# Four modulation slabs of each layer: out of the attention block, into the norm ahead of the FFN

## What is computed

```python
def layer(x, cond, p, l, angles, ctx):
    mod = jax.nn.silu(cond) @ p['w_mod'][l] + p['b_mod'][l]
    sh1, sc1, g1, sh2, sc2, g2 = jnp.split(mod, 6, axis=-1)
    h = rms_norm(x, p['norm1'][l]) * (1.0 + sc1) + sh1
    mixed, ctx_out = token_mixers(h, p, l, angles, ctx)
    x = x + g1 * mixed
    h = rms_norm(x, p['norm2'][l]) * (1.0 + sc2) + sh2
    a, u = jnp.split(h @ p['w_ffn_in'][l], 2, axis=-1)
    x = x + g2 * ((jax.nn.silu(a) * u) @ p['w_ffn_out'][l])
    return x, ctx_out
```

## Time and profile before

| | |
|---|---|
| median of 3 runs | 2581.82 us (2580.06 to 2582.97) |
| the profiled execution | 2584.01 us, its span 2582.1 us |
| PE busy | 2415.1 us, 94% of the span |
| DVE / ACT / POOL busy | 54% / 37% / 18% |
| mean granted clock of PE | 0.968 of full speed |
| read from HBM | 206.46 MB, 82 GB/s over the span |

### The profile page before, as it was taken

How to read it: one execution, slowest core, us unless ns; L and a number is a source line. 1 busy time by engine, 2 the same in 40 slices (tenths; PEclk the granted TensorE clock), 3 DMA queues, 4 the chain that set the end, 5 groups by cost and what they waited for, 6 DMA issues and landing times. The chain is left out here.

```text
span 2582.1 us, 40460 instructions
## 1 busy us (share of the span) xinstructions
PE 2415.1 (94%) x16718; PEld 2237.5 (87%) x16718; DVE 1402.1 (54%) x2040; ACT 943.2 (37%) x1747; POOL 476.2 (18%) x345
## 2 busy tenths in 40 slices
PE   6988989999999899999999799898999989999997
PEld 5767867789999899999997588677999989999997
DVE  3334657642225783866753446676222368568383
ACT  3433346631113442333335233675111234234240
POOL 1241000000003531403335010000000055033130
PEclk9989999999999899999989899999999999999998
DMA  7233233222222132232220521311222222313221
GB/s 217 91 113 125 67 95 128 75 74 74 74 82 82 34 98 67 72 100 59 82 91 19 177 92 38 125 37 34 82 75 80 67 61 71 98 50 98 66 78 62
DMA packets 246197, 213.52 MB, mean 83 GB/s; under 512 B 8928, under 2 KB 231712, under 8 KB 246016
## 3 DMA queue, kind: packets, MB, share of 16 engines
q1 hardware_dynamic: 239696, 208.10, 26.2%
q10 hardware_dynamic: 5808, 2.17, 0.4%
q0 software_dynamic: 512, 0.66, 0.2%
HBM read 206.46 MB, written 4.46 MB: 82 GB/s over the span
## 5 line engine op out<-in xcount | busy, mean ns | idle before, releaser
L2516 DVE TENSOR_TENSOR ring_low<-raw,ring_high 128x512 fp32r<-128x512 f32 (+1 forms) x278 | 268.8, 989 | 102.4 <-ACT ring_high L2413 102.2
L2413 ACT ACTIVATE ring_high<-raw 128x512 fp32r<-128x512 f32 (+1 forms) x278 | 156.8, 609 | 253.3 <-PE ps L2657 211.8
L1537 DVE TENSOR_TENSOR wL<-raw,wH 128x1024 fp32r<-128x1024 f32 (+1 forms) x46 | 79.8, 1736 | 287.4 <-ACT wH L1474 286.7
L2705 PE MATMUL ps<-hH,ring_low 128*128 128x320 f32 x640 | 199.5, 312 | 4.8 <-issue 4.8
L2705 PE MATMUL ps<-hL,ring_high 128*128 128x320 f32 x640 | 199.0, 311 | 0.0
L2705 PE MATMUL ps<-hH,ring_high 128*128 128x320 f32 x640 | 198.9, 311 | 0.0
L332 PE MATMUL ps<-wH,hL 128*128 128x512 f32 (+1 forms) x460 | 175.6, 382 | 14.7 <-DVEq L998 14.7
L2657 PE MATMUL ps<-gH,ring_low 128*128 128x320 f32 x704 | 165.2, 317 | 18.2 <-DVE gL L2548 18.2
L369 PE MATMUL ps<-hH,wL 128*128 128x320 f32 x768 | 177.9, 313 | 0.0
L369 PE MATMUL ps<-hL,wH 128*128 128x320 f32 x768 | 176.0, 310 | 0.0
L369 PE MATMUL ps<-hH,wH 128*128 128x320 f32 x768 | 175.7, 310 | 0.0
(11 more groups left out here) (328 smaller groups left out, 6089.9 us busy)
## 6 DMA issues: line engine op xcount, KB each, us to landing
raw<-in_w_in SPq DMA_DIRECT2D x56, 1024.0 KB, 5.3
raw<-in_w_ffn_in SPq DMA_DIRECT2D x88, 512.0 KB, 5.0
modw<-in_w_mod SPq DMA_DIRECT2D x24, 1024.0 KB, 5.1
gmod<-in_w_mod SPq DMA_DIRECT2D x16, 1024.0 KB, 7.6
raw<-in_w_ffn_out SPq DMA_DIRECT2D x16, 1024.0 KB, 5.1
raw<-in_w_branch SPq DMA_DIRECT2D x24, 512.0 KB, 3.4
head_w<-in_w_mod SPq DMA_DIRECT2D x8, 1024.0 KB, 11.8
raw<-in_w_out SPq DMA_DIRECT2D x8, 1024.0 KB, 5.6
```

Source lines behind the costliest of these rows:

```text
L1537: nc.vector.tensor_tensor(m.wL[:, slot, 0:n], m.raw[:, slot, 0:n], m.wH[:, slot, 0:n].bitcast(F32), ALU.subtract).then_inc(m.sem("low_read ...
L2413: nc.scalar.activation(ring_block(m.ring_high, b, src.shape[1], src.shape[2]), src, ACT.Copy).then_inc(m.sem("w_high"), 1)
L2516: nc.vector.tensor_tensor(ring_block(m.ring_low, b, nk, cols), src, ring_block(m.ring_high, b, nk, cols).bitcast(F32), ALU.subtract).then_ ...
L2705: last = nc.tensor.matmul(m.ps[:, plan.banks[n, i][0], 0:HALF], w[:, k, :], a[:, k, :], start=(k == 0 and q == 0), stop=(k == 3 and q == 2))
```

## The change

Of the 8 slabs of its own layer that an attention block computed, it now computes 4 (16 to 19, the rest of sh2 and sc2); those of the next layer stay. Slabs 20 to 23 (g2) are loaded at the start of the tail into four buffers of their own (`fmod`), by SP ahead of slab 2 of w_out, and are multiplied by PE inside the norm: two ahead of the sums over channels, two between these and the spread. ACT copies the two rows of results (`f_row`) ahead of and behind its root. PE turns them by 8 small matmuls behind the last tile of slab 4, DVE adds the bias ahead of its first FFN multiplication, and PE waits for that addition before the second tile of slab 5.

```diff
@@ tail, sync @@
             for j in range(2):
                 sp.sem_inc(m.sem(f"slab_loaded{j}"), 16)
+            for j in range(4):
+                sp.dma_start(m.fmod[j][:, :, :], k_tiles(d["w_mod"], L, (20 + j) * W256, W256)
+                             ).then_inc(m.sem(f"mod_loaded{j}"), 16)
             for n in range(2, N):
@@ attention @@
-    mods = [(L, 16 + j) for j in range(8)] + ([(L + 1, j) for j in range(8)] if more else [])
+    mods = [(L, 16 + j) for j in range(4)] + ([(L + 1, j) for j in range(8)] if more else [])
@@ tail, scalar, norm @@
+                def mod_row(p):
+                    act.wait_ge(m.sem("slab_used"), 2 * p + 2)
+                    nc.scalar.activation(m.f_row[:, p, :], m.ps[:, plan.banks[4, 0][p], :], ACT.Copy
+                                         ).then_inc(m.sem("mod_rows"), 1)
+
+                if j == 0:
+                    mod_row(0)
                 b = plan.banks["norm", j][1]
                 act.wait_ge(m.sem("sums_done"), j + 1)
                 nc.scalar.activation(m.n_st[:, 0:5], m.ps[:, b, 256:261], ACT.Sqrt,
                                      bias=m.cst[:, K_LAM + 4:K_LAM + 5]).then_inc(m.sem("std"), 1)
+                if j == 0:
+                    mod_row(1)
@@ tail, vector, slab 4 @@
+                    if f == 0:
+                        dve.wait_ge(m.sem("mod_turned"), 1)
+                        add_mod_bias(nc, m, L, plan.banks["norm", 0][1], 40, 8, 264).then_inc(m.sem("mod_added"), 1)
                     dve.wait_ge(m.sem("silu"), f + 1)
@@ tail, tensor, norm @@
+                def mods(p):
+                    for i in (2 * p, 2 * p + 1):
+                        pe.wait_ge(m.sem(f"mod_loaded{i}"), 16)
+                        mod_groups(nc, m, m.fmod[i], plan.banks[n, 0][p], i % 2 * W256).then_inc(m.sem("slab_used"), 1)
+
+                if j == 0:
+                    wait_free((n, 0))
+                    mods(0)
                 wait_free(("norm", j))
...
                 last.then_inc(m.sem("sums_done"), 1)
+                if j == 0:
+                    mods(1)
                 pe.wait_ge(m.sem("rstd"), j + 1)
                 spread_rstd(nc, m, b, [c * P for c in range(TT)]).then_inc(m.sem("rstd_spread"), 1)
                 for c in range(2):
                     wait_free((n, c))
+                if j == 0:
+                    pe.wait_ge(m.sem("mod_rows"), 2)
...
+                if j == 0:
+                    for t in range(8):
+                        last = nc.tensor.matmul(m.ps[:, b + 1, 264 + 2 * t:266 + 2 * t],
+                                                m.f_row[:, t // 4, t % 4 * P:(t % 4 + 1) * P], m.sel[:, :],
+                                                start=True, stop=True)
+                    last.then_inc(m.sem("mod_turned"), 1)
@@ tail, tensor, slab 5 @@
                         wait_free((n, c))
+                        if n == 5 and c == 1:
+                            pe.wait_ge(m.sem("mod_added"), 1)
```

More of the change, by code:

```diff
@@ L225, in __init__ @@
         self.gL = at("gL", [P, 8, T], x0 + 20480, F32R)
+        self.fmod = [at(f"fmod{j}", [P, KT, W256], x) for j, x in enumerate((x0, x0 + 20480, x1, x1 + 8192))]
+        self.f_row = at("f_row", [P, 2, 512], x0 + 51200)
         self.n_x0 = at("n_x0", [P, 4, T], x0 + 10240)
```

## The result

The changed kernel takes 2593.69 us (median of 5 runs, 2591.67 to 2596.72), the kernel before 2581.82, so the medians are 11.9 us apart. The ratio over all runs is 1.0055, 95% interval 1.0040 to 1.0071, which is 14 us. It is slower by 1.7 to 2.1 times what was forecast (+6.8 us). Timed once more it was 1.0045 (1.0029 to 1.0061), 11.6 us. The profiled execution after has a span of 2589.8 us against 2582.1.

The account below looks back on a forecast made before the run. The prediction took the kernel as bound by TensorE (PE), busy for 94% of the span. Attention -8.6, OUT's stall +8.8, clock +3.0 and norm +3.6 summed to +6.8 on the median 2581.82: 2588.6 us, range 2579 to 2596.

Parts of the forecast that it names:

- The clock behind the stall: OUT, behind PE's wait for slab 2: clock falls to half for some 3 us; +3.0 both layers, bounds 0 and 3.4.
- Rival (1): OUT: the clock holds after the stalls, all else as forecast, giving 2585.6; chance 0.18.
- The stall: OUT: four loads ahead delay slab 2, PE waits 4.1 in L0, 4.7 in L1; +8.8, bounds +7.4 and +11.
- the two ways: L0's slab 2 landing: 16.5 after 799.51 (816.0) from attention's four loads, or 816.8 from its earlier 804.67 plus 12.1.
- rival 2: OUT: slab 2 is served beside the four loads, on time, so no stall or clock loss; 2576.8, chance 0.08.
- 3.0 a load: Tail's load queue: 1.05 MB at 347 GB/s adds 3.0 us.
- the place and the releaser of the wait: PE waits 4 to 5 us on DVE's ring_low, some 14 us into OUT, behind ACT's wait for w_out.
- Attention: Attention blocks lose slabs and turns: 3.6 shorter in L0, 5.0 in L1; -8.6, bounds -7.2 and -11.8.
- Rival (4): Attention gives all the removed PE work, -11.8 instead of -8.6, clock as forecast; 2585.4, chance 0.12.
- The norm: Second norm with added slabs: spread ends 2.0 later in L0, 1.3 in L1; +3.6 with bias, bounds +1 and +9.
- The turn and the bias: Behind slab 4: turn's 1.9 of PE covered by waits of 1.29 and 2.42; bias addition costs 0.15 a layer.
- Rival (3): Behind the norm: turn uncovered (+3.8), L1's slab 2 later (+1.9), ACT's copies 0.5 a layer; 2595.3, chance 0.17.

Follow-up runs that it names:

- again: The changed kernel, unaltered, timed and profiled once more beside the kernel before: 2591.98 us, ratio 1.0045.
- loads_only: The kernel before plus only the four 1 MB loads ahead of slab 2 of w_out, their data unread: 2594.59 us, ratio 1.0061 to the kernel before.
- fill_stall: The kernel before plus the four loads, with PE multiplying the loaded slabs between slabs 1 and 2 of w_out, results unused: 2588.65 us, ratio 1.0038.
- hold_slab3: The kernel before plus the four loads ahead of slab 2, with SP holding slab 3's load until slab 2 has landed: 2594.83 us, ratio 1.0061.
- late_loads: The changed kernel with its four loads issued behind slab 3 of w_out instead of ahead of slab 2: 2573.88 us, 0.9978 of the kernel before.
- three_ahead: The changed kernel with three loads ahead of slab 2 of w_out and the fourth behind slab 3: 2581.66 us, 1.0002 of the kernel before.
- slab2_alone: The kernel before with SP holding slab 3's load until slab 2 has landed, no added loads: one execution, 2580.84 us beside 2579.66.

## Why the forecast was wrong

The direction and the mechanism were right, the size was not: +6.8 against 9.3 to 10.4 in the stages and 11.6 to 14 in the timings. The measured 2593.69 lies inside the range of 2579 to 2596, but above the forecast's own 2585 to 2592. Step by step:

- **The clock behind the stall, +3.0: the step that failed most.** OUT exceeds its wait by 2.99 and 2.78 (changed), 2.44 and 1.86 (again), 2.13 and 3.00 (loads_only), together 4.3 to 5.8 for both layers, and fill_stall takes 1.9 and 2.7 of it away. I took half of a low spell of 3 us from the start of L0's attention. There the clock fell when PE came back and was low until 365.3, nearer 3.5; here the low clock lasted until 819.5, 5.9 us after PE's return at 813.61, and half of that is 2.95. My upper bound for both layers, 3.4, was too low. A longer spell stood in the same trace of the kernel before, at the start of L1's attention, where PE came back at 1623.31 from an idle of 5.11:

```profile
1626.00:1628.00 2.00, 1.95 (x7) 1.00 (x4) 1.36 (x2) 0.62 (x1) 0.00 (x0) 0.50 1.08 371
1628.00:1629.00 1.00, 0.00 (x0) 0.00 (x0) 1.00 (x1) 1.00 (x4) 0.00 (x0) 0.92 1.09 354
```

  It lasted until about 1628.2, 4.9 us after PE's return, and half of that in each layer would have given 4.9. Rival (1), a clock that holds, fell. Why one spell lasts 3.4 us and another 5.9 stays open.
- **The stall, +8.8:** measured 5.62 + 4.37 = 9.99 and 5.68 + 4.29 = 9.97. L1 was within 0.4, L0 1.5 too short. In L0 ACT was released 18.5 us after the start of the tail, where the two ways had 16.5 and 17.3. In hold_slab3 the bulk of the bytes ended when the sum said and the release waited for a trailing share; the sum had no term for that. L1 was in part luck: the same four loads cost 5.72 there in loads_only and 5.79 in hold_slab3. That the loads stand in line and slab 2 waits for all four was right (rival 2 fell), and so were "3.0 a load" and the place and the releaser of the wait.
- **Attention, -8.6:** -9.5 to -10.9, so another 1 to 2 better. L1's -5.0 is -4.8. In L0 I took 3.6 from L1's eight steps, 5.2 came: L1's wait of 1.28 and the step that starts at 1753.91 make its eight steps 2.3 us longer than L0's are now. That they belong to L1, because its conversion of the next weights stands there, is read from the order and not tested. I had named this and discounted it too little. Rival (4)'s 11.8 wasn't reached.
- **The norm, +3.6:** with what is behind it +4.4, +6.0 and, in late_loads, +2.8. The delay of the spread was worked out at 2.0 and 1.3 and came as 1.7 to 3.3 and 0.8 to 2.5, by whether the clock held. That it would hold with the gaps filled was right in half the cases; why it fell in the others stays open.
- **The turn and the bias:** forecast 0 and 0.15 a layer; measured 0.08 to 0.16. The cover by the two waits was read rightly. Rival (3) fell with it, though its time, 2595.3, is the nearest to what was measured: its causes, an uncovered turn and a later slab 2 in L1, didn't come, and the number was luck.

On the two main steps the sum is short by 1.3 to 2.8 (the clock) and 1.2 (the stall), on the norm by 0.8 to 2.4; attention gives back 1 to 2.

The Trainium skill ("DMA: Bandwidth & Descriptors", Queues, rings and completion order) says that on each SDMA engine descriptors are consumed in ring order. The runs agree: with one load fewer ahead of slab 2 (three_ahead) ACT is released 15.45 us after the start of the tail instead of 18.51 in L0, and 14.28 instead of 17.25 in L1, 3.0 less in each.

## What to carry to other kernels

A load has a place in a queue as an instruction has: when work is moved to a stage, ask first which transfer its own loads now stand in front of, and issue them behind whatever is wanted first. Here that one line is the difference between 0.5% slower and 0.2% faster. When you price an idle of PE, add the time at the lower clock behind it, and take for its upper bound the longest spell that the trace shows (here 4.9 us), not the nearest (3.5). And when you work out a landing as bytes over rate, add a margin for the last bytes, which can trail the bulk: the release came 0.6 to 2.7 us behind it here.

## What the runs showed of the hardware

- A wait of PE of 2.56 us in the middle of dense work brought the clock down to 0.50 for 3.4 us, beginning 1.2 us after PE was back at work. Waits of 5.62 and 4.37 brought it down before PE was back, and it stayed low for another 5.9 and 5.5 us. A wait of 1.40 brought no fall, nor did 1.65 and 2.08 in fill_stall, where slabs that write 32 rows at a time had kept PE busy ahead of them; the granted clock was 1.00 through both.
- In the norm the clock fell behind gaps of only 0.86 and 0.58 (spread of 1.86 in L0 and 2.50 in L1 of the kernel before), and with these filled by slabs it still fell in half the cases (L1 of the changed kernel: 2.40). So the length of the last wait alone doesn't say whether it falls.
- ACT began about 0.5 us after the last bytes of a load. In L1 of slab2_alone, where nothing was queued ahead, and in hold_slab3, behind four loads, about one engine's share (0.07, 25 GB/s) ran on for 1.4 to 2.2 us when the bulk was over, so that ACT began 2.7 and 1.9 us behind the bulk; in L0 of slab2_alone it was 0.6. Which engine trails, and why, wasn't tried.
